# Parts of a gated tile's three sums made a round later, and the final norm's statistics per token in columns of 96

## The reference, cut to what matters

```python
h2 = _rmsnorm(x, g_fn)
gt, up = jnp.split(h2 @ w_fi, 2, axis=-1)
x = x + (jax.nn.silu(gt) * up) @ w_fo
y = _rmsnorm(x, g_final)      # x * rsqrt(mean(x*x) + EPS) * g_final, per token
```

## Time and profile before

| | us |
|---|---|
| median of 3 runs | 981.95 (981.93 to 981.97) |
| the profiled execution, its own time | 981.5 |
| its span, first to last instruction | 980.0 |
| PE, DVE, ACT, POOL busy | 937.4, 779.6, 465.7, 123.2 |
| round 0's P1 begins | 626.9 |
| round 26's P1 begins | 909.3 |
| the last product ends | 961.4 |

### The profile page before, as it was taken

The page is one execution under the profiler, slowest core; times in us unless marked ns, Lnnn a source line. Parts: engine busy times, 40 slices in busy tenths (PEclk is TensorE's granted clock), DMA queues, the critical chain, the costliest instruction groups (busy, mean ns, idle before and its releaser), DMA issues. The chain is left out here.

```text
span 980.0 us, 18425 instructions
## 1 busy us (share of the span) xinstructions
PE 937.4 (96%) x6830; PEld 913.2 (93%) x6830; DVE 779.6 (80%) x1219; ACT 465.7 (48%) x679; POOL 123.2 (13%) x116
## 2 busy tenths in 40 slices
PE   5999989999999999999999999999999999999992
PEld 5999979999999999999999999999999999999892
DVE  6875778698779859796445569899888999899996
ACT  5643335346334524453833345355445554555562
POOL 4133042006002300510212000000000000000002
PEclk9988989999999999999999999999999999999997
DMA  6226511620451152124242222232222222322212
GB/s 188 87 65 146 93 44 55 236 86 22 160 173 65 45 223 86 43 96 131 89 159 87 81 69 87 87 118 96 89 86 88 86 95 81 127 87 86 87 44 96
DMA packets 25091, 97.26 MB, mean 99 GB/s; under 512 B 6816, under 2 KB 6960, under 8 KB 20672
## 3 DMA queue, kind: packets, MB, share of 16 engines
q1 hardware_dynamic: 23280, 78.01, 24.8%
q0 software_dynamic: 1744, 18.42, 6.1%
HBM read 84.03 MB, written 12.39 MB: 98 GB/s over the span
## 5 line engine op out<-in xcount | busy, mean ns | idle before, releaser
L1215 PE MATMUL ps<-h_hi,w_hi 128*128 128x288 f32 x896 | 194.3, 298 | 1.5 <-DVE w_lo L1586 1.5
L1215 PE MATMUL ps<-h_lo,w_hi 128*128 128x288 f32 x896 | 192.1, 296 | 0.0
L1215 PE MATMUL ps<-h_hi,w_lo 128*128 128x288 f32 x896 | 192.0, 296 | 0.0
L767 ACT ACTIVATE w_hi<-raw 128x1024 fp32r<-128x1024 f32 x76 | 80.3, 1057 | 188.5 <-PE ps L1215 175.7
L1215 PEld LDWEIGHTS ps<-h_hi,w_hi 128*128 128x128 f32 x896 | 143.6, 189 | 3.5 <-issue 2.8
L1215 PEld LDWEIGHTS ps<-h_hi,w_lo 128*128 128x128 f32 x896 | 144.8, 189 | 0.0
L1215 PEld LDWEIGHTS ps<-h_lo,w_hi 128*128 128x128 f32 x896 | 144.6, 189 | 0.0
L1586 DVE TENSOR_TENSOR w_lo<-raw,w_hi 128x1024 fp32r<-128x1024 f32 x76 | 95.3, 1254 | 59.9 <-ACT w_hi L767 59.7
L1801 DVE SCALAR_TENSOR_TENSOR conv<-a_p,vec,conv x120 | 96.9, 807 | 0.2
L1487 PE MATMUL ps<-cols_b,late 128*128 128x288 f32 x432 | 63.8, 296 | 4.9 <-ACT tmp L1065 4.5
L1487 PEld LDWEIGHTS ps<-cols_b,late 128*128 128x128 f32 x432 | 58.8, 188 | 6.6 <-issue 5.9
(11 more groups left out here) (338 smaller groups left out, 1888.5 us busy)
## 6 DMA issues: line engine op xcount, KB each, us to landing
raw<-w_head_in SPq DMA_DIRECT2D x40, 512.0 KB, 3.5
raw<-w_fp_in SPq DMA_DIRECT2D x18, 1024.0 KB, 4.9
cs<-st_c_in POOLq DMA_DIRECT2D x4, 2048.0 KB, 9.7
c_s_out<-cs POOLq DMA_DIRECT2D x4, 2048.0 KB, 7.7
raw<-w_fo_in SPq DMA_DIRECT2D x8, 1024.0 KB, 4.8
x<-xT_in SPq DMA_DIRECT2D x16, 288.0 KB, 4.3
raw<-w_cgcv_in SPq DMA_DIRECT2D x8, 512.0 KB, 3.6
raw<-w_ga_in SPq DMA_DIRECT2D x8, 512.0 KB, 3.6
```

The lines of the kernel that those rows point to most:

```text
L767: act.activation(w_hi[:, s, :], raw[:, s, :], ACT.Copy).then_inc(hi_ready, 1)
L1215: last = pe.matmul(ps[:, 2 * s + b, 0:HALF], wt[:, w, k * P:k * P + P], src[:, k, b * HALF:b * HALF + HALF], start=(k == 0 and wt is w_hi ...
```

## The change

1. The hi and lo parts of a second tile's three sums are made one round later: on ACT behind `snap_u3(i-1)`, on DVE between `sum_2(i)` and `sum_4(i)`.
2. In every round DVE makes `lo_s1_s3` before `lo_s2`; before it was the other way round (except in the last turn).
3. In the last turn the last tile's sums are added and split one column block at a time, behind `lo_s2`; P6 waits for the nT2 block only and P7 for nT3.
4. In the last round ACT runs a one-column square root first, ahead of `snap_u3(28)`, so that the table of the square root is loaded there. The gain of rows 4 and 5 is applied later, and for rows 6 and 7 it is part of DVE's product.
5. P3(29) comes before P4(29). The squares of the last two rows are made by halves. The mean squares are computed per token: 96 tokens of squares are the stationary side and one column of 1/D the moving one, three columns of 96 to a half. The root and the reciprocal are then of 3 columns. The result is put on the diagonal of a matrix and spread to all partitions by a matmul with ones, once for DVE, which multiplies from PSUM, and once for POOL through ACT's copy. The right half goes first, then the left.
6. y is stored by halves of rows, in 7 transfers from SP and ACT instead of 8 from SP.

```diff
+CH = 96
+NCH = HALF // CH
+Y_RIGHT_DVE, Y_RIGHT_POOL = (3, 4, 5, 6, 7), (0, 1, 2)
+Y_LEFT_DVE, Y_LEFT_POOL = (3, 4, 5, 6, 7, 2), (0, 1)
...
# SP's stores (ACT has three more: rows 0-2 right, row 2 left, rows 0-1 left)
+            store(y_ready, 3, 3, 3, 1)
+            store(y_ready, 5, 6, 2, 1)
+            store(y_ready, 7, 3, 2, 0)
+            store(y_ready, 10, 5, 3, 0)
...
# ACT, the rounds
+                if i == NR - 1:
+                    steps.settle()
+                    steps.on(act.activation(warm[:, :], eps[:, :], ACT.Sqrt))
                 if i:
                     snap_u3(i - 1)
+                if i >= 2 and is_in(i - 2) and place_of(i - 2)[0] == "second" and i - 1 != OUT_AT[LAST_G]:
+                    second_sums_tile_hi(i - 2)
...
                         second_tile_hi(i - 1)
-                        second_sums_tile_hi(i - 1)
...
# ACT, the end
             snap_u3(NR - 1)
-            row_squares(KT - 2, KT)
-            row_squares(KT - 1, KT)
-            deviation(3, sum_done, 3)
+            end_square(1, 0, 0)
+            row_gain(KT - 4)
+            row_gain(KT - 3)
+            end_square(2, 1, 1)
+            end_square(3, 0, 1)
+            token_deviations(0)
+            end_square(4, 1, 0)
+            copy_rstd(0, 1)
+            token_deviations(1)
+            for c in range(NCH):
+                act.wait_ge(tok_rstd_ready, 2)
+                act.activation(diag[:, 1, c, :], ident[0:CH, 0:CH], ACT.Copy, scale=tok[:, 1, 1, c:c + 1])\
+                    .then_inc(diag_ready, 1)
+            copy_rstd(1, 0)
...
# PE, the end
+            def token_means(n, b, r):
+                pe.wait_ge(sq_added, SQ1 + 2 * KT)
+                pe.wait_ge(sq_ready, 3 * KT + 1 + n)
+                for c in range(NCH):
+                    at = b * HALF + c * CH
+                    pe.matmul(ps[0:CH, n, c:c + 1], acc[:, at:at + CH], mean_d[:, 0:1], start=True, stop=False)
+                    last = pe.matmul(ps[0:CH, n, c:c + 1], sqs[:, r, at:at + CH], mean_d[:, 0:1], start=False, stop=True)
+                last.then_inc(sum_done, 1)
+            def spread(n, to):
+                pe.matmul(ps[:, to, 0:HALF], mean_c[0:CH, :], diag[:, n, :, :].rearrange("p c t -> p (c t)"),
+                          start=True, stop=True).then_inc(spread_done, 1)
+            p3(NR - 1)
             p4(NR - 1)
-            p3(NR - 1)
-            mean(3, mean_d, acc, sum_done)
+            token_means(0, 1, 0)
+            spread(0, 6)
+            spread(0, 2)
+            token_means(1, 0, 1)
+            spread(1, 7)
+            spread(1, 2)
...
# DVE, the last turn
                 end_tile_left(i - 1)
+                second_sums_tile_lo(i - 2)
                 gate_right(i - 1)
                 sum_4(i)
                 end_tile_left_lo(i - 1)
+                lo_s2(i)
                 end_tile_right(i - 1)
-                second_tile_sums(i - 1)
-                lo_s2(i)
-                end_sums_tile_lo(i - 1)
+                end_tile_sums(i - 1)
...
# DVE, the other rounds
                 sum_2(i)
+                if i >= 2 and is_in(i - 2) and place_of(i - 2)[0] == "second" and i - 1 != OUT_AT[LAST_G]:
+                    second_sums_tile_lo(i - 2)
                 sum_4(i)
...
-                lo_s2(i)
+                lo_s1_s3(i)
                 if is_out(i - 1):
                     x_of_p4(i - 1)
-                lo_s1_s3(i)
+                lo_s2(i)
...
# DVE, the end
+            reciprocals(0)
+            dve.tensor_tensor(diag[:, 0, :, :], ident[...], tok[:, 1, 0, :]..., ALU.mult).then_inc(diag_ready, 1)
+            products(0, 1, Y_RIGHT_DVE[0:3])
+            reciprocals(1)
+            products(0, 1, Y_RIGHT_DVE[3:])
+            products(1, 0, Y_LEFT_DVE)
```

More of the change, by code:

```diff
@@ L609, in _, with store @@
                 sp.dma_start((raw0, raw1)[i % 2][:, 0:4 * half_of(i) * P], src).then_inc(chunk_loaded[i % 2], 16)
[L611 to L617, removed]
+            def store(sem_, count, first, n, b):
+                sp.wait_ge(sem_, count)
+                at = slice(b * HALF, b * HALF + HALF)
+                sp.dma_start(y[:, first:first + n, at], x[:, first:first + n, at]).then_inc(y_stored, 16)
+            store(y_ready, 3, 3, 3, 1)
+            store(y_ready, 5, 6, 2, 1)
+            store(y_ready, 7, 3, 2, 0)
+            store(y_ready, 10, 5, 3, 0)
+            sp.wait_ge(y_stored, 16 * 7)
         @block.gpsimd
@@ L742, in _ @@
                     .then_inc(mlo_ready, 1)
[L745 to L754, removed]
+            pool.wait_ge(cstat_done, 2)
+            pool.memset(mean_c[:, :], 1.0).then_inc(consts_ready, 1)
+            pool.wait_ge(xfin_ready, KT - 2)
+            for n, (rows_, at) in enumerate(((Y_RIGHT_POOL, slice(HALF, T)), (Y_LEFT_POOL, slice(0, HALF)))):
+                pool.wait_ge(rs_ready, 4 + n)
+                for k in rows_:
+                    pool.tensor_tensor(x[:, k, at], x[:, k, at], rs[:, at], ALU.mult).then_inc(y_pool_ready, 1)
         @block.scalar
@@ L1531, in p6 @@
                 of_second(i, second_sums_lo)
-                product(i, "P6", "nS2", "nT2", 0, False, of_last(i, end_sums_lo))
+                product(i, "P6", "nS2", "nT2", 0, False, of_last(i, second_sums_lo, SECONDS[LAST_G]))
             def p5(i):
@@ L2178, in second_tile_sums @@
                 dve.wait_ge(second_sum, 2 * seconds_before(i) + 1)
[L2179 to L2180 removed]
+                dve.tensor_tensor(hid_a32[:, 4, 1, k, :], hid_b32[:, 0, 1, k, :], hid_a32[:, 2, 1, k, :], ALU.add)\
                     .then_inc(second_sum, 1)
@@ L2406, in _, with add_end_square @@
-            for b in range(2):
-                half = rs[:, b * HALF:(b + 1) * HALF]
-                dve.reciprocal(half, half).then_inc(rs_ready, 1)
-            dve.wait_ge(rs_ready, 5)
-            dve.wait_ge(xfin_ready, KT)
-            for k in range(Y_POOL, KT):
-                dve.tensor_tensor(x[:, k, :], x[:, k, :], rs[:, :], ALU.mult).then_inc(y_ready, 1)
+            last = NR - 1
+            def add_end_square(n, r, b):
+                dve.wait_ge(sq_ready, 3 * KT - 2 + n)
+                at = slice(b * HALF, b * HALF + HALF)
+                dve.tensor_tensor(acc[:, at], acc[:, at], sqs[:, r, at], ALU.add).then_inc(sq_added, 1)
@@ new lines, in reciprocals, with products @@
+            def reciprocals(n):
+                dve.wait_ge(tok_dev_ready, n + 1)
+                dve.reciprocal(tok[:, 1, n, :], tok[:, 0, n, :]).then_inc(tok_rstd_ready, 1)
+            def products(n, b, rows_):
+                dve.wait_ge(spread_done, 2 * n + 1)
+                at = slice(b * HALF, b * HALF + HALF)
+                for k in rows_:
+                    if k < KT - 2:
+                        ins = dve.tensor_tensor(x[:, k, at], x[:, k, at], ps[:, 6 + n, 0:HALF], ALU.mult)
+                    else:
+                        ins = dve.scalar_tensor_tensor(x[:, k, at], x[:, k, at], vcol(V_GFIN + k), ps[:, 6 + n, 0:HALF],
+                                                       ALU.mult, ALU.mult)
+                    ins.then_inc(y_ready, 1)
@@ new lines, in _ @@
+            dve.wait_ge(p_done["P5"], last + 1)
+            dve.tensor_tensor(x_half(last, 1, 1), x_half(last, 1, 1), bank_of(last, 2), ALU.add).then_inc(mid_read, 1)
+            add_row_square(KT - 4)
+            add_row_square(KT - 3)
+            dve.wait_ge(x_p2, outs_before(last + 1))
+            dve.wait_ge(snapped, 3 * last + 2)
+            dve.tensor_tensor(x[:, KT - 2, :], x[:, KT - 2, :], hf[:, last % 2, :], ALU.subtract).then_inc(end_x, 1)
+            dve.wait_ge(mid_read, last + 1)
@@ new lines, in _ @@
+            dve.wait_ge(snapped, 3 * last + 3)
+            dve.tensor_tensor(x_half(last, 1, 1), x_half(last, 1, 1), tmp[:, last % 2, 0:HALF], ALU.add)\
+                .then_inc(end_x, 1)
+            dve.wait_ge(sq_added, SQ1 + 2 * KT - 2)
+            add_end_square(1, 0, 0)
+            dve.wait_ge(end_x, 2)
+            dve.wait_ge(p_done["P3"], last + 1)
+            dve.tensor_tensor(x_half(last, 0, 1), x_half(last, 0, 1), bank_of(last, 2), ALU.subtract).then_inc(end_x, 1)
+            add_end_square(2, 1, 1)
```

129 lines of the change are left out of this document (85 added, 44 removed).

## The result

The changed kernel takes 976.35 us in the median of 15 runs (969.9 to 979.7), beside 981.95 for the kernel before on the same chip (980.8 to 984.4): ratio of the means 0.9934, 95% interval 0.9918 to 0.9951. So it is 5.6 us less by the medians and 6.5 us less by the means (4.8 to 8.1). I had forecast 978.8, in 976.4 to 981.4: the direction was right, the gain was about twice the 3.15 that I had said, and the median lies just outside the range. The profiled execution took 974.41 us, its span 972.8.

A forecast was written before the change was run, and what follows sets the result against it. PE works 96% of the span, so only its pauses (mainly ACT's `snap_u3`, DVE's list right behind) and the tail could give time: -0.3 - 0.1 - 0.1 + 0.2 - 1.8 + 0.95 - 2.0 = -3.15 us, to 978.8, range 976.4 to 981.4.

The forecast's parts named there:

- Rounds 0 to 5: First rounds: P4's stalls of 0.78 become P6 stalls of 0.39, round 0 loses 0.74; about -0.3 us.
- a full second round goes at 11.51 us: Ordinary rounds: DVE's list, no shorter, sets 11.51 us where PE wants 11.12, so P6 stalls 0.39.
- Rounds 12 to 19: Rounds 12 to 15 gain 1.2, the swapped order costs 0.4 in 16 to 18 and 0.75 in 19; sum -0.1.
- rounds 23 to 25: Three rounds of 34.27 us in all become 11.12 plus twice 11.51; -0.1 us.
- Last turn: P1(26) to P1(27): falls from 14.57 to 12.8 us, P7's wait for `snap_u2` stays; -1.8 us.
- Table: Last round: the early table load delays `snap_u3(28)`, so PE stands about 0.95 us before P4(28); +0.95, bounds 0 and 1.5.
- P4 last and its wait gone: Round 29: P3 needs no snap, the wait of 0.59 goes; P4 ends at 960.6 instead of P3 at 961.4.
- The tail behind the last product: Last product to span end: columns and halves end the span at 978.0 instead of 980.0; -2.0 us.
- 12 passes of 0.12: Token means in the tail: 6 matmuls in 12 passes of 0.12 us each, 0.24 at half clock, 2.9 for the left.
- full clock through the tail: Rival: small matmuls keep PE's clock at 1.00, left means 1.45 us less, spread 0.7 less; 977.0 in all; chance 0.17.
- All of the 5.6 us come back: Rival, ordinary rounds: DVE's order has unseen slack, P6 never waits; 3.3 us more, 975.5; chance 0.07.
- P6 late everywhere, slower: Rival: `lo_s2` behind `lo_s1_s3` makes P6 late, 0.35 in 20 rounds, 7 us; 985.5; chance 0.09.

The follow-up runs named there:

- E8: Changed kernel with DVE making the moved lo part of a second tile's sums behind the fourth sum instead of ahead of it; 978.66 us, ratio 0.9953.
- E3: Changed kernel with DVE making `lo_s2` ahead of `lo_s1_s3` again in the ordinary rounds; 972.79 us, ratio 0.9898 to the kernel before.
- E4: Changed kernel without the early one-column square root, so the table loads where the token deviations need it; 975.23 us, ratio 0.9928 to the kernel before.
- E6: Changed kernel with both `lo_s2` ahead of `lo_s1_s3` again and no early square root; 971.26 us, ratio 0.9885 to the kernel before.
- E5: Kernel before with the new last turn alone; rounds, order of the lo parts and tail old; 981.94 us against 983.43, ratio 0.9995.
- E7: E6 with 20 extra PE products in the tail that nobody reads (4, 7 and 9); 967.25 us, ratio 0.9843 to the kernel before.
- E2: Kernel before with the new last round and tail alone (early table load, P3 first, halves, columns of 96); 978.56 us, ratio 0.9963.
- E9: E7 without the nine extra products behind the left half's token means, 11 left; 971.15 us, ratio 0.9886 to the kernel before.

## Why the prediction was half right

The mechanisms were those that I named. Two terms were mis-sized, and both errors went the same way; the forecast's sum was -3.15, the profiles' like for like is -6.1.

- *Rounds 0 to 5, forecast -0.3, measured -0.94.* P6 waits for `lo_s2` as said, and round 0 loses 0.75 (I had 0.74). The step that failed is "a full second round goes at 11.51 us". I had added up distances of starts from a trace in which the fourth sum stood 0.12 behind its place because it needs the second sum's result, and took the 0.12 for work. The moved lo part fills it (E8). The other 0.04 of the 0.16 no run isolates; I had taken off 0.25 for the pause ahead of `lo_s2`, but there its start stood 0.94 behind the fourth sum's and in E3, where it doesn't wait, stands 0.60 behind it, so the pause was 0.34. The round is 11.35 and PE's loss 0.23, not 0.39. Over rounds 2 to 5 that is 0.64, the whole difference, of which E8 shows 0.49.
- *Rounds 12 to 19, -0.1 against -0.36; rounds 23 to 25, -0.1 against -0.44.* The same term, twice more. The costs of the swapped order were right: 0.32 in rounds 16 to 18 (I had 0.4), 0.64 in round 19 (0.75), 0.21 in round 27 by E4 against E6 (0.2).
- *Last turn, -1.8 against -1.79.* The number is right, but by luck in part: I had put it to part 3 alone, and E5 shows 0.8 for that; the other 1.0 needs the moved sums.
- *Table, +0.95 against +0.80* by E4. Right in place and kind. That the load would cost nothing in the tail I didn't see.
- *P4 last and its wait gone, -0.84 against -0.83* (P1(27) to round 29, before against E6).
- *The tail behind the last product, forecast 17.4, measured 15.9.* The step that failed is "12 passes of 0.12", doubled to 2.9 us at half clock. The price came from a matmul of another shape; one column wide, a pass starts 0.085 after the one before at full clock and 0.16 at half. That makes the right means 0.4 us shorter and the left ones 1.1, and all behind them moves with them: left means' end 6.0 after the last product instead of 7.6. Hand-overs, root, reciprocal, diagonal and the product from PSUM (L2504, three in 1.18, so 0.37 apart; the one at 967.76, beside POOL, took 0.45 from start to end, as one alone) were as priced, and the stores moved 370 to 381 GB/s in packets of 1152 bytes (968 to 971 us).
- *The clock.* I gave full clock through the tail 0.17 and 1.8 us. E7 shows 1.8 us (15.90 to 14.11), but only with the extra products; the small matmuls alone didn't hold the clock in any profile.
- *"All of the 5.6 us come back", 0.07.* It is what E3 shows for rounds 2 to 5: P6 never waits there, with 11.29 us of DVE in rounds of 11.12. My argument against it was a rate; with only two to four such rounds together, what counts is the slack. In the changed kernel the swap takes this slack away.
- *P6 late everywhere, slower.* Its place was right, its price was the 3.1 us of E3, paid inside a gain. (The 985.5 should have been 985.8, 7 us above 978.8.)

What stays open: executions of one kernel lie up to 10 us apart. The tail's clock accounts for some 2 us of it (tails of 15.0 to 16.8 without fillers). More lies before P1(0), which began between 621.8 and 630.3 us in twelve profiles without a change of code there. In three of them (E2, E4, E6) the third stretch of granted clock 0.50 lay at 112 to 114 us and P1(0) came at 621.8 to 624.0; in the nine others it lay at 130 to 134 and P1(0) at 625.8 to 630.3. Windows (granted clock third from the end), kernel E4, then kernel after:

```profile
104.00:116.00 12.00, 9.96 (x64) 9.73 (x63) 6.61 (x13) 6.56 (x14) 0.00 (x0) 0.86 0.48 118
```

```profile
128.00:140.00 12.00, 8.45 (x58) 8.10 (x59) 10.98 (x19) 4.32 (x8) 4.03 (x4) 0.86 0.16 46
```

What sets where it lies wasn't tried, nor whether it delays P1(0) or only goes with it. Nor do the runs say why the forecast's own 0.45 between median and profile was 1.9 for the changed kernel; with such a spread one profile can't.

## What to carry to other kernels

An engine whose list is longer than the round doesn't set the time as long as the slack between its results and their use covers the lag for the few rounds in a row; so put first what is used first, and count slack, not rates. When distances between starts are added up, take out those that a dependency made, since the next order fills them. In a tail of small matmuls the TensorE clock is a term of its own: a few products that nobody reads, in PE's waits, were worth 0.9 to 2.7 us here by the profiles (14.11 against 14.96 and 16.83).

## What the runs showed of the hardware

The granted clock fell to 0.50 between 2.7 and 5.3 us after the last product in the nine kernels without fillers, though PE had small matmuls in between; with 20 fillers in PE's waits it held for 11.8 and 12.5 us, well beyond PE's last matmul (7.8), and with 11 of them for 5.8 (E9). The fillers took 3.3 us of PE in all (0.69, 1.16, 1.44).

A table load runs ahead of its activation's wait: in E4 it began at 953.97 with the means not yet begun, and hid behind them.

One kernel's stores dragged. Windows at the end of kernel E8 (clock, DMA share, GB/s last):

```profile
974.00:976.00 2.00, 0.00 (x0) 0.00 (x0) 0.00 (x0) 0.00 (x0) 0.00 (x0) 0.50 1.05 371
976.00:979.00 3.00, 0.00 (x0) 0.00 (x0) 0.00 (x0) 0.00 (x0) 0.00 (x0) 0.50 0.06 19
```

The last 1.8 us of it move 20 to 26 GB/s: a DMA share of 0.06, as of one of 16 DMA engines at work and the others done. Among these stores the queue for instructions (kind "instruction") has one packet of 16 KB, from 971.8 to 973.7; it fell among the stores in this profile only, and in the other profiles of the new tail it came 1.5 to 4.3 us after the last product or after 16 us. That it held up this engine's stores is likely by the times, not shown by a run.
